# First chunk of the two gated feed-forward layers: hidden rows turned by VectorE blocks and ScalarE moves instead of TensorE transposes

## What is computed

```python
def swiglu(h, w_gu, w_down):
    gate, up = jnp.split(h @ w_gu, 2, axis=-1)
    return (jax.nn.silu(gate) * up) @ w_down

h = swiglu(rms_norm(x, ffn1_pre[l]), ffn1_w_gu[l], ffn1_w_down[l])   # f0
x = x + 0.5 * rms_norm(h, ffn1_post[l])
...                                                                  # token mixer
h = swiglu(rms_norm(x, ffn2_pre[l]), ffn2_w_gu[l], ffn2_w_down[l])   # f1
```

## Time and profile before

| | us |
|---|---|
| median of 3 runs | 959.77 (959.74 to 959.83) |
| the profiled execution | 959.8 |
| its span in the profile | 958.0 |
| TensorE busy | 946.4 |
| VectorE busy | 653.0 |
| ScalarE busy | 601.6 |
| mean granted TensorE clock | 0.999 |

### The profile page before, as it was taken

How to read it: one execution, slowest core, us unless ns; L and a number is a source line. 1 busy time by engine, 2 the same in 40 slices (tenths; PEclk the granted TensorE clock), 3 DMA queues, 4 the chain that set the end, 5 groups by cost and what they waited for, 6 DMA issues and landing times.

```text
span 958.0 us, 14710 instructions
## 1 busy us (share of the span) xinstructions
PE 946.4 (99%) x5439; PEld 816.2 (85%) x5439; DVE 653.0 (68%) x822; ACT 601.6 (63%) x1035; POOL 80.2 (8%) x105
## 2 busy tenths in 40 slices
PE   9999999999999999999999999999999999999997
PEld 7888888787888888888889789889899899999996
DVE  5655556676666555557679798786566677777776
ACT  6677777566667767686557596554454475555544
POOL 4300000010110000000100913000000010000000
PEclk9999999999999999999999999999999999999999
DMA  9955656543346565555545253244652536464641
GB/s 317 297 198 183 201 177 217 176 151 135 110 158 239 175 215 179 200 194 176 183 133 198 77 178 134 89 158 145 223 178 89 176 125 227 155 207 163 212 139 44
DMA packets 110179, 166.03 MB, mean 173 GB/s; under 512 B 5748, under 2 KB 84884, under 8 KB 110004
## 3 DMA queue, kind: packets, MB, share of 16 engines
q1 hardware_dynamic: 108104, 160.45, 49.9%
q0 software_dynamic: 1872, 4.93, 1.7%
q10 hardware_dynamic: 160, 0.07, 0.0%
HBM read 164.38 MB, written 1.05 MB: 173 GB/s over the span
## 4 chain that ended last, share of the span: by engine, by line
PE 93%; DVE 3%; ACT 3%; issue 1%; DMA 0%; POOLq 0%; POOL 0%; ACTq 0%; DVEq 0%
PE ps L2170 28%; PE ps L2172 28%; PE ps L2171 28%; PE ps L2213 1%; PE ps L2892 1%; PE ps L2565 1%; PE ps L2194 1%; PE ps L2548 1%; ACT arena L840 1%; PE ps L2828 0%; DVE spare_lo L1398 0%; DMA rows_f<-in_ffn_pre 0%; PE ps L2263 0%; ACT w_hi L642 0%; PE ps L2264 0%
## 5 line engine op out<-in xcount | busy, mean ns | idle before, releaser
L1398 DVE TENSOR_TENSOR w_lo<-raw,w_hi 128x2048 fp32r<-128x2048 f32 (+2 forms) x142 | 321.6, 2274 | 91.1 <-ACT w_hi L642 91.0
L642 ACT ACTIVATE w_hi<-raw 128x2048 fp32r<-128x2048 f32 (+2 forms) x142 | 267.1, 1889 | 70.5 <-PE ps L2172 61.1
L2170 PE MATMUL ps<-w_hi,xT_hi 128*128 128x512 f32 (+2 forms) x722 | 275.1, 381 | 0.6 <-DVE w_lo L1410 0.5
L2172 PE MATMUL ps<-w_hi,xT_lo 128*128 128x512 f32 (+2 forms) x722 | 270.8, 375 | 0.0
L2171 PE MATMUL ps<-w_lo,xT_hi 128*128 128x512 f32 (+2 forms) x722 | 270.3, 374 | 0.0
L2170 PEld LDWEIGHTS ps<-w_hi,xT_hi 128*128 128x128 f32 x722 | 135.9, 188 | 26.0 <-issue 1.8
L2172 PEld LDWEIGHTS ps<-w_hi,xT_lo 128*128 128x128 f32 x722 | 135.8, 188 | 24.5
L2171 PEld LDWEIGHTS ps<-w_lo,xT_hi 128*128 128x128 f32 x722 | 136.0, 188 | 22.6
L2170 PE MATMUL ps<-xT_hi,w_hi 128*128 128x256 f32 x448 | 127.0, 284 | 0.0
L2172 PE MATMUL ps<-xT_hi,w_lo 128*128 128x256 f32 x448 | 126.8, 283 | 0.0
L2171 PE MATMUL ps<-xT_lo,w_hi 128*128 128x256 f32 x448 | 126.8, 283 | 0.0
(11 more groups left out here) (356 smaller groups left out, 1117.4 us busy)
## 6 DMA issues: line engine op xcount, KB each, us to landing
raw<-in_ffn_w_gu SPq DMA_DIRECT2D x84, 512.0 KB, 4.6
raw<-in_ffn_w_down SPq DMA_DIRECT2D x44, 512.0 KB, 3.9
raw<-in_w_ffn_up SPq DMA_DIRECT2D x44, 512.0 KB, 4.8
raw<-in_w_in SPq DMA_DIRECT2D x34, 512.0 KB, 4.6
raw<-in_w_out SPq DMA_DIRECT2D x24, 512.0 KB, 4.4
raw<-in_w_ffn_down SPq DMA_DIRECT2D x22, 512.0 KB, 4.2
raw<-in_w_mem_k SPq DMA_DIRECT2D x8, 512.0 KB, 4.1
raw<-in_w_mem_v SPq DMA_DIRECT2D x8, 512.0 KB, 4.2
```

The costliest lines, as they stand in the source:

```text
L642: act.activation(w_hi[HOME[k]][:, 0:n], raw[k % RING][:, 0:n], ACT.Copy).then_inc(rounded, 1)
L1398: TTn(w_lo[HOME[k]][:, 0:n], raw[k % RING][:, 0:n], w_hi[HOME[k]][:, 0:n].bitcast(F32), ALU.subtract).then_inc(resid, 1)
L2170: pe.matmul(out_, lh, rh, start=first, stop=False, **kw)
L2172: return pe.matmul(out_, ll, rh, start=False, stop=last, **kw)
```

## The change

The hidden rows of chunk 0 of f0 and f1 are made in the way of chunks 1 to 9. Eight transposes of 128 x 128 (four for each layer) go from TensorE; VectorE gets one block transpose for each layer; ScalarE gets 16 moves for each layer and reads `h_raw` in SBUF where it read PSUM. TensorE still waits for `s_ready` of both row tiles in `gate_up` of chunk 1, now at the head of each row tile. The argument `between` goes; `turn` is left for the convolution layer alone, as `turn_up`. The count `turned_n` of the block transposes is shifted by one for each layer. ScalarE's wait on `unit_used` ahead of `hT_hi` is left out for chunk 0, as no earlier down product reads that tile.

```diff
         def turned_n(fc):
-            return fc // NCH * (NCH - 2) + fc % NCH
+            return fc // NCH * (NCH - 1) + fc % NCH + 1
...
-                elif peeled == 0:
-                    act.wait_ge(hT_ps, f + 1)
-                    act.activation(hT_hi[:, :, :].rearrange("p a b -> p (a b)"), ps[:, 2, :],
-                                   ACT.Copy).then_inc(hT_hi_done, 1)
                 else:
                     act.wait_ge(h_turned, j + turned_n(fc))
...
                     act.wait_ge(h_moved, j + turned_n(fc))
-                    act.wait_ge(unit_used, 3 * j + (k + 3))
+                    if peeled != 0:
+                        act.wait_ge(unit_used, 3 * j + (k + 3))
...
-                    if peeled not in (0, NCH - 1):
+                    if peeled != NCH - 1:
                         turn_blocks(2 * j + (2 * fc + 2))
...
-                elif peeled == 0:
-                    dve.wait_ge(hT_hi_done, j + (hT_n(fc) + 1))
-                    TTn(hT_lo[:, :, :].rearrange("p a b -> p (a b)"), ps[:, 2, :],
-                        hT_hi[:, :, :].rearrange("p a b -> p (a b)").bitcast(F32), ALU.subtract).then_inc(hT_lo_done, 1)
...
-                        if between is not None and half == 0 and t == 1:
-                            between()
...
-                    gate_up(u + 2, 0, lambda: turn(f, conv, 0, 0))
+                    gate_up(u + 2, 0, 2 * f * NCH)
```

More of the change, by code:

```diff
@@ L359, in two_blocks @@
             "ssq_done", "rstd_done", "scaled", "xt_ps", "xt_hi", "xt_lo"))
-        (gu_ps, silu_done, s_ready, hT_ps, hT_hi_done, hT_lo_done) = map(sem, (
-            "gu_ps", "silu_done", "s_ready", "hT_ps", "hT_hi_done", "hT_lo_done"))
+        (gu_ps, silu_done, s_ready, hT_hi_done, hT_lo_done) = map(sem, (
+            "gu_ps", "silu_done", "s_ready", "hT_hi_done", "hT_lo_done"))
         (end_hT_ps, end_hT_hi, end_hT_lo, half_done) = map(sem, (
@@ L2363, in narrow, with gate_up @@
                 return last
-            def gate_up(k, j, between=None, s_before=None):
+            def gate_up(k, j, s_before=None):
                 for half in range(2):
@@ L2442, in conv_up, with turn_up @@
                     last.then_inc(unit_used, 1)
[L2444 to L2459, removed]
+            def turn_up():
+                for t in range(TT):
+                    pe.wait_ge(up_ready, t + 1)
+                    for q in range(4):
+                        last = pe.transpose(ps[:, 2 + q // 2, q % 2 * S + t * P:q % 2 * S + t * P + P],
+                                            act_in[:, t, q * P:q * P + P], ident)
+                last.then_inc(uT_ps, 1)
             def small_columns():
@@ L2477, in feed_forward @@
                     factor_row()
-                    turn(f, conv, 0, 0)
+                    turn_up()
                     conv_up(u + 2, 0, 1)
@@ L2488, in feed_forward @@
                     else:
-                        gate_up(u + 5, j, None, 2 * (f * NCH + 1))
+                        gate_up(u + 5, j, 2 * (f * NCH + 1))
                     down(u + 7, j, n_hT + 2, False)
@@ L2495, in feed_forward @@
                 else:
-                    gate_up(u + 3 * NCH - 4, 0, None, 2 * (f * NCH + NCH - 2))
+                    gate_up(u + 3 * NCH - 4, 0, 2 * (f * NCH + NCH - 2))
                 k9, k10 = u + 3 * NCH - 2, u + 3 * NCH - 1
```

## The result

| | before | after |
|---|---|---|
| median (us) | 959.74 (959.69 to 959.97, 7 runs) | 963.05 (962.72 to 963.54, 7 runs) |
| the profiled execution | 959.8 | 963.05 |
| its span | 958.0 | 961.3 |
| start of the last matmul | 950.99 | 953.27 |
| from there to the end of the span | 7.0 | 8.0 |

The ratio is 1.0034 [1.0025, 1.0043]: slower by 3.3 us. The sign is as forecast, the size is not: I had said 2.1 us more, and at most 3.0. The last two lines of the table divide the 3.3 us in two: 2.28 us have come by the last matmul, 1.0 us comes behind it.

A forecast was written before the change was run, and what follows sets the result against it. TensorE, busy 946.4 of 958.0 us, was taken as the bound. Down products 0.94 and 0.93 us later plus 2 x 0.10 restart made 2.07 us, the 0.98 gain included; on 959.8 that gives 961.9 us, range 960.9 to 962.8.

The forecast's parts named there:

- The gain of the transposes: TensorE ahead of down(u + 4) in f0 and f1: dropping four transposes gives back 0.48 and 0.50 us, 0.98 in all.
- The rival that counted ScalarE's 5.11 us of moves against 0.48 us of TensorE: Chunk 0: VectorE's block transpose is not the cheap way, as ScalarE must make whole tiles; no chance of its own given.
- The chain on ScalarE and the two waits: Chunk 0, f0 and f1: 7.46 us on ScalarE before the split of u+4 makes TensorE wait 1.42 us per layer.
- the sum of 2.07: Down products of f0 and f1: starts 0.94 and 0.93 us later, plus 2 x 0.10 us of slower restart.
- the signs that I gave for the moves and the split: Expected in f1's changed profile: first move near 281.3 us, split of u+4 near 287.0 us.
- What is late next: Chunk 1 of f0: the rest of u+7 comes later but with 2.6 us to spare; costed at nothing.
- the slack covers it: Rival: u+4 comes in time in f0 and f1, leaving only the gain, 958.8 us; 4%.
- swallowed at the wait: Rival: TensorE's existing wait between 176 and 184 us takes up f0's delay, 960.8 us; 8%.
- a second wait: Rival: late DMAs of u+7 and u+8, or VectorE, make TensorE wait again in f0's chunk 1; 962.9 us; 9%.
- the delay is on the chain that ended last, so I let it through in full: From the down products to the program's end: the 2.07 us arrives whole, 1.8 us outside the span unchanged, giving 961.9 us.
- The clock: Rival: TensorE's clock falls in the new wait, costing 5.4 us over one down product, some 967 us; 2%.

The follow-up runs named there:

- run 1: Changed kernel with split and rest of unit u+4 put ahead of the 16 moves in f0 and f1: 959.92 us, ratio 0.9999.
- run 6: Changed kernel with unit u+4 split ahead of the moves in f0 and f1, plus 24 small VectorE instructions at the start: 959.01 us, ratio 0.9991.
- run 2: Kernel before with two small VectorE instructions added at the start: 960.89 us, ratio 1.001.
- run 4: Changed kernel with 24 small VectorE instructions added at the start: 962.18 us, ratio 1.0024.
- run 3: Kernel before with 31 small ScalarE instructions added at the start: 960.08 us, ratio 1.0001.
- run 5: Kernel before with 24 small VectorE instructions added at the start: 960.07 us, ratio 1.0002.
- run 8: Changed kernel with 24 small VectorE instructions and four further ScalarE moves behind the 16 in chunk 0 of f0 and f1: 966.48 us, ratio 1.0076.
- run 9: The kernel of run 8 measured again, unchanged: 967.61, 967.85, 966.02 and 966.21 us, ratio 1.0071.

## Why the prediction was right, and where it fell short

**The gain of the transposes: right.** I took 0.98 us for the eight; with the waits gone, the last matmul came 0.96 us earlier (run 1), and the time fell by 0.9 us (run 6). Counted from the split of u+3 in f0 the gain is 1.03 and 1.10 us. The Trainium skill (TensorE: Matmul & The Clock Gate, Part 4: PE-mode transpose) gives about 275 ns for a transpose of 128 x 128 in bf16. Eight of them would be an estimated 2.2 us; the runs do not agree with it as a cost on the path of these float32 transposes, which is 0.12 us for one. The rival that counted ScalarE's 5.11 us of moves against 0.48 us of TensorE was right about the work and not about the time: in run 6 the moves stand where they make nobody wait, and the kernel is faster without the transposes.

**The chain on ScalarE and the two waits: right.** Split of u+4 expected at 28.69, seen at 28.83; moves 5.08 us as in the earlier trace rows; the down product 33.20 - 21.38 = 11.82 us behind the split of u+3, where I had 32.97 - 21.23 = 11.74, so that TensorE starts it 1.53 us later than it could, where I had 1.42; restart 0.08 us where I had 0.10. By the last matmul the delay is 2.28 us. Of it 0.15 stands already at the split of u+3 (21.38 for 21.23), ahead of every edit; over all profiled executions of this study that moment lies between 21.16 and 21.74 us. The other 2.13 answer to the sum of 2.07. For f1 the signs that I gave for the moves and the split (281.3 and 287.0) left out f0's delay of 1.04 us; with it the split is expected at 288.0, and it was seen at 288.20.

**What is late next: right.** No wait at the down product of chunk 1 (49.65 us, 1.30 later than the earlier trace rows), and f0's delay is found again in f1, whose split of u+3 is at 280.74, 1.21 later than in the earlier trace rows. The rivals "the slack covers it", "swallowed at the wait" and "a second wait" are thereby out; run 1 shows how little lay between the first of them and the truth, a matter of two lines of order.

**The step that failed** is "the delay is on the chain that ended last, so I let it through in full [...] the 1.8 us outside the span unchanged". The delay did come through in full to the last matmul. But the sentence takes what is behind the last matmul, 7.0 us, as a constant, and that was 8.0. I had costed the edit by the instructions that it moves, and had never asked what the number of instructions itself changes. Of the 1.2 us by which the forecast fell short, 1.0 is this term, 0.15 the later start of f0's split and 0.06 the chain. The term depends on two added instructions of VectorE: run 2 switches it on and run 4 off, run 3 shows that 31 on ScalarE do not matter, run 5 that the padding itself does not. The range was made of the uncertainties inside the one stretch and of its rivals, with nothing for the rest of the program, and so was too narrow above. The trace of before could have warned me: the same fetch lies 1.9 us behind its last write.

**The clock.** The rival was right to be small for this change: waits of 1.36 us left the clock alone, as the wait of 1.47 us had suggested. But its price was wrong. I wrote 5.4 us for one fall, as if it lasted for a whole down product; it lasts about 3.4 us and costs about 1.5 (runs 8 and 9): about eight matmuls start 0.43 us apart in it, where I had let 24 do so. And the change stands nearer to it than I had thought: four more moves of 0.3 us are enough.

## What to carry to other kernels

Work that is handed to an engine with plenty of idle time is priced by what is queued behind it: here 5.1 us of ScalarE's moves ahead of one weight split cost more than the transposes gave, and the same moves behind that split cost nothing, with 0.2 us to spare. Where a change of a microsecond is judged, read the tail of the trace too, the last write and the instruction fetches around it, and test a pair of kernels with some padding instructions on each engine before the difference is put down to the edit. A gain that an experiment shows up to the last matmul may still be missing at the end of the program.

## What the runs showed of the hardware

- **An instruction fetch competes with the output's DMAs.** A fetch of 8 KB during the last writes goes with one of the 16 DMA engines finishing about 1.0 us after the others (slowest landing 3.3 or 3.4 us for 2.3 or 2.4), in all three kernels where it fell there (after, runs 1 and 2) and in none of the nine other traces. Two more VectorE instructions moved it in, from 8.16 to 5.05 us behind the last matmul; with 24 it stood some 16 us ahead. So it hangs on VectorE's code; the rule for the point at which a fetch is made was not tested. The fetch itself is recorded at 0.65 us after, 0.55 in run 2 and 0.32 in run 1, for the same loss each time: how it costs a full microsecond stays open.
- **The clock behind a wait of TensorE.** With dense work before and behind, waits of 1.36, 1.95 and 1.99 us left the granted clock at 1.00. With four waits of 2.58 to 2.62 us, three times about 3.4 us at 0.50 began between 0.4 us before and 1.2 us after the end of the wait, and once none did, in the same program and with the same work around it. What decides between them stays open. Such a stretch costs 1.3 to 1.7 us (936.09 of run 8 is 4.16 above the 931.93 of run 4, of which the longer waits are 2.5) and makes the times of one kernel fall in two groups.
- **A wait grows one for one.** 0.63 and 1.26 us of further moves on ScalarE made 0.6 and 1.2 to 1.3 us more of wait on TensorE, two engines further on.
